# A fused transformer block on one core: five steps of 128, 128, 256, 256 and 256 tokens in place of four steps of 256

## What is computed

```python
xn = _rmsnorm(x, mix_norm_w[l]); proj = xn @ w_in[l]        # q, k, v, gates ...
o_da = diff attention, o_gla = gated linear attention, o_xa = attention over mem
merged = g0 * (o_da @ w_br_da) + g1 * (o_gla @ w_br_gla) + g2 * (o_xa @ w_br_xa)
x = x + merged @ w_out[l]
q = xb @ w_q; s = q . sub_keys; top_s, top_i = top_k(s, 16)   # per head, two halves
best_s, best_j = top_k(cand_s, 16); idx = ...; g = softmax(best_s)
u = expert_u[idx]; v = expert_v[idx]
act = gelu(einsum('thkd,td->thk', u, xb))
x = x + einsum('thk,thkd->td', g * act, v)
```

## Time and profile before

| | |
|---|---|
| median of 3 runs | 3866.09 us (3856.25 to 3876.32) |
| the profiled execution | 3867.53 us |
| its span, first to last instruction | 3865.7 us |
| mean granted TensorE clock | 0.862 |
| busy, share of span | PE 75%, PEld 38%, DVE 59%, ACT 17%, POOL 30% |
| weight blocks loaded | 360 of 512.0 KB |
| read from memory and written | 1286.51 MB and 12.58 MB |

### The profile page before, as it was taken

The page is one execution under the profiler, slowest core; times in us unless marked ns, Lnnn a source line. Parts: engine busy times, 40 slices in busy tenths (PEclk is TensorE's granted clock), DMA queues, the critical chain, the costliest instruction groups (busy, mean ns, idle before and its releaser), DMA issues. The chain is left out here.

```text
span 3865.7 us, 31929 instructions
## 1 busy us (share of the span) xinstructions
PE 2892.5 (75%) x11208; PEld 1470.0 (38%) x11208; DVE 2281.4 (59%) x5605; ACT 674.8 (17%) x1244; POOL 1146.2 (30%) x1044
## 2 busy tenths in 40 slices
PE   6779886789988857779987765787897854555555
PEld 3458652335645312335644322333563521111111
DVE  1230187775445786775454777676555598665665
ACT  1220111531111111531111111441111000000000
POOL 0000003343332233433332233343332324443442
PEclk9779997889998978989998887898999966777777
DMA  4114449999999898899999898889999969999998
GB/s 154 68 60 153 169 134 383 359 410 384 398 410 374 353 353 347 346 377 376 399 391 355 333 350 352 333 344 350 384 418 368 398 266 379 421 421 389 420 421 367
DMA packets 212159, 1301.22 MB, mean 337 GB/s; under 512 B 25360, under 2 KB 26144, under 8 KB 80928
## 3 DMA queue, kind: packets, MB, share of 16 engines
q0 software_dynamic: 149760, 1082.20, 69.7%
q1 hardware_dynamic: 62240, 216.99, 15.1%
HBM read 1286.51 MB, written 12.58 MB: 336 GB/s over the span
## 5 line engine op out<-in xcount | busy, mean ns | idle before, releaser
L582 POOL DMA_INDIRECT rowbuf<-in_peer_uv,idx x848 | 943.2, 1112 | 2266.6 <-PE acc L844 1542.9
L844 PE MATMUL acc<-rowbuf,diag 128*64 128x512 f32 x3392 | 1010.6, 707 | 474.3 <-DVE diag L1474 471.3
L1464 DVE CUSTOM_DVE_ANT_0 rowbuf<-rowbuf,xr 128x1024 f32<-128x1024 f32 x848 | 1021.3, 1223 | 529.1 <-DMA rowbuf<-in_peer_uv,idx 525.3
L844 PEld LDWEIGHTS acc<-rowbuf,diag 128*64 128x64 f32 x3392 | 246.1, 154 | 1053.9 <-DVE diag L1474 581.1
L1086 ACT ACTIVATE acts<-dots 128x2 f32<-128x2 f32 x512 | 104.1, 203 | 2476.3 <-DVE dots L1464 2416.8
L640 PE MATMUL bank<-xnT,W 128*128 128x256 f32 x1792 | 413.4, 387 | 0.0
L1474 DVE TENSOR_SCALAR diag<-consts,acts,gw 128x64 f32<-128x64 f32 x1024 | 285.6, 351 | 182.1 <-ACT acts L1086 109.1
L626 PE MATMUL bank<-W,xnT 128*128 128x512 f32 x832 | 384.7, 612 | 3.1 <-DVE xnT L1174 2.6
L640 PEld LDWEIGHTS bank<-xnT,W 128*128 128x128 f32 x1792 | 340.1, 193 | 98.7 <-issue 54.2
L844 PE MATMUL acc<-kv,diag 128*64 128x512 f32 x560 | 210.9, 780 | 115.7 <-DVE diag L1474 108.5
L640 PE MATMUL bank<-arena,W 128*128 128x256 f32 x1024 | 242.3, 394 | 45.9 <-DMA W<-in_w_blocks 43.4
(11 more groups left out here) (165 smaller groups left out, 2297.2 us busy)
## 6 DMA issues: line engine op xcount, KB each, us to landing
W<-in_w_blocks SPq DMA_DIRECT2D x360, 512.0 KB
rowbuf<-in_peer_uv,idx POOLq DMA_INDIRECT x848
xs<-in_x SPq DMA_DIRECT2D x16, 512.0 KB, 9.6
xr<-x SPq DMA_DIRECT2D x32, 256.0 KB, 7.9
out_y<-xs SPq DMA_DIRECT2D x8, 512.0 KB, 7.4
x<-arena SPq DMA_DIRECT2D x8, 512.0 KB
fin<-out_y POOLq DMA_DIRECT2D x8, 512.0 KB
out_y<-fin POOLq DMA_DIRECT2D x8, 512.0 KB, 10.2
```

Of the source, the lines that this page charges most:

```text
L582: pool.indirect_dma_start(rows[SLOT[g]], None, a["peer_uv"], bass.IndirectOffsetOnAxis(ap=idx[:, at // NB, at % NB:at % NB + 1], axis=0)). ...
L844: mm = pe.matmul(acc[HP * j:HP * (j + 1), h * HALF:(h + 1) * HALF], diag[:, c % DIAGS, j, :], v[:, D + h * HALF:D + (h + 1) * HALF], start ...
L1464: dve.tensor_tensor_reduce(out=u, in0=u, in1=xr[:, t, j, :], scale=1.0, scalar=0.0, op0=ALU.mult, op1=ALU.add, accum_out=dots[:, c % QS, j ...
```

## The change

The step sizes become a list, `TILES = (1, 1, 2, 2, 2)` tiles, and everything that was counted as `NT * (n - 1)` or `T` is counted by `tiles(n)`, `tile0(n)` and `ntok(n)`. The same eight tiles are mixed, ranked and gathered in the same order, with the same number of gathers, pairs and rankings. What differs:

- the first 256 tokens are two steps of 128. A step of one tile has half the attention units, chunks, streams of `token_major`, and streams 128 columns instead of 256 in `channel_major`; there are as many weight blocks in it as in a step of 256;
- the rows of tile 0 are used while tile 1 is mixed, those of tile 1 while tiles 2 and 3 are mixed; from there on a step of 256 is mixed beside the 256 gathers of the step before, as it was;
- `spread()` halves the lengths of the places in `BY_TOKENS` for a step of one tile, and starts at `GQK` of the next step behind a step that has no second ranking;
- the ring has one row buffer more for tile 0, and for tiles 2 to 7 as many as it had for them;
- ScalarE waits at `WQ` 0 for the stores of both tiles of `x2`, where it waited for one at `WQ` 0 and one at `WQ` 1.

```diff
+TILES = (1, 1, 2, 2, 2)
+STEPS = len(TILES)
...
+def tiles(n):
+
+    return TILES[n - 1] if n else NT
...
+def tile0(n):
+
+    return sum(TILES[:n - 1])
...
+    if n < STEPS:
+        kv, kt, q, rest = front(n + 1)
+        out += kv + ranks[0][:2] + kt + ranks[0][2:] + q
+        return out + (ranks[1][:2] + rest + ranks[1][2:] if tiles(n) > 1 else rest)
+    return out + sum(ranks, [])
...
 def row_buffers(g):
+    n = step_of(g)
     if n == STEPS:
         return [*range(ROWS, ROWS + EXTRA), *range(ROWS)]
-    return list(range(ROWS)) + kv[n + 1 if rel < KV_UNTIL else n + 2:]
+    share = (g - 2 * pair0(n)) / (tiles(n) * NB)
+    kv = [ROWS + i for i in range(KV_ROWS) if kv_step(i) > n + 2 or kv_step(i) == n + 2 and share < KV_UNTIL]
+    return list(range(ROWS)) + kv
...
+BY_TOKENS = ("GQK", "XQ", "GV", "GR", "GATE", "BR", "WO", "WQ", "SC", "K", "V", "Q", "OT", "GO", "SU")
...
+    def span(p):
+        return SPAN[p[0]] * (tiles(p[1]) / NT if p[0] in BY_TOKENS else 1)
+
+    def start(m):
+        if tiles(m) > 1:
+            return places.index(("R", m, 1, 0))
+        return places.index(("GQK", m + 1)) if m < STEPS else len(places)
...
+        count = tiles(m + 1) * PAIRS if m + 1 < STEPS else LAST_RANK
...
             def token_major(job, out_of):
-                    for t in range(NT):
+                    for t in range(tiles(job[1])):
...
             def channel_major(job, rhs):
+                nk = ntok(job[1])
...
-                        mm = pe.matmul(ps[:, c * T:(c + 1) * T], w[:, k, :], rhs[:, k, :], start=k == 0, stop=k == KC - 1)
+                        mm = pe.matmul(ps[:, c * nk:(c + 1) * nk], w[:, k, :], rhs[:, k, 0:nk], start=k == 0, stop=k == KC - 1)
...
                 for j in range(4):
                     if j == 2 and n < STEPS:
                         square_x(n + 1)
-                    if j < 2:
-                        act.wait_ge(x2_out[j], 16 * n)
-                    copy(("WQ", n, j), qp[:, j % 2, :], 1024)
+                    if j == 0:
+                        for g in range(tile0(n), tile0(n + 1)):
+                            act.wait_ge(x2_out[g % NT], 16 * (g // NT + 1))
+                    copy(("WQ", n, j), qp[:, j % 2, 0:4 * ntok(n)], 4 * ntok(n))
...
                 begin(n)
-                rank(n, 1)
+                if tiles(n) > 1:
+                    rank(n, 1)
```

More of the change, by code:

```diff
@@ L237, in kv_released @@
 def kv_released(n):
-    g = [g for g in range(GATHERS) if SLOT[g] == ROWS + n - 1 and step_of(g) < STEPS]
+    mine = [ROWS + i for i in range(KV_ROWS) if kv_step(i) == n]
+    g = [g for g in range(GATHERS) if SLOT[g] in mine and step_of(g) < STEPS]
     return g[-1] // 2 + 1 if g else 0
@@ L259, in spread @@
     for m, (at, end) in enumerate(zip(starts, starts[1:] + [len(places)])):
-        total = sum(SPAN[p[0]] for p in places[at:end])
-        count = NT * PAIRS if m + 1 < STEPS else LAST_RANK
+        total = sum(span(p) for p in places[at:end])
+        first = pair0(m + 1)
+        count = tiles(m + 1) * PAIRS if m + 1 < STEPS else LAST_RANK
         so_far = 0
         for p in places[at:end]:
-            SINCE[p] = NT * PAIRS * m + count * so_far / total
-            so_far += SPAN[p[0]]
-            BEFORE[p] = NT * PAIRS * m + count * so_far / total
+            SINCE[p] = first + count * so_far / total
+            so_far += span(p)
+            BEFORE[p] = first + count * so_far / total
 spread()
@@ L591, in x1_back, with store @@
                 pool.dma_start(fin[:, :], y_tiles[g]).then_inc(fin_in, 16)
-            def store(n, t):
-                g = NT * (n - 1) + t
+            def store(g):
                 pool.wait_ge(y_ready, g + 1)
                 pool.dma_start(y_tiles[g], fin[:, :]).then_inc(y_out, 16)
[L598 to L611, removed]
+            for g in range(SEQ // P):
+                if g == tile0(STEPS):
+                    pool.wait_ge(*filled(("WQ", STEPS, 3)))
+                pool.wait_ge(route_done, g + 1)
+                for k in range(NB):
+                    if k == ROWS:
+                        if g:
+                            store(g - 1)
+                        x1_back(g)
+                    gather(NB * g + k)
+            store(SEQ // P - 1)
         @block.tensor
@@ L668, in project_front @@
                 channel_major(("GQK", n), xnT)
-                for t in range(NT):
+                for t in range(tiles(n)):
                     turn(("QT", n, t), [qn[:, t, 2 * h:2 * h + 2, :].rearrange("p a b -> p (a b)") for h in range(DA_H)],
@@ L1228, in memory_attention @@
+                dve.tensor_tensor(flat(gkd(n)), flat(gkd(n)), flat(gqk(n)[:, 2:4, :]), ALU.mult).then_inc(gla_ops, 1)
             def memory_attention(n):
-                for t in range(NT):
+                for t in range(tiles(n)):
                     job = ("XS", n, t)
@@ L1368, in route @@
                 picks.upto(("WO", n, 1))
-                after(norm_rows(2 * n + 1))
-                for t in range(NT):
+                after(norm_rows(2 * n + 1, tiles(n)))
+                for t in range(tiles(n)):
                     dve.scalar_tensor_tensor(xn2[:, t, :], xs[:, t, :], st2[:, 4 + t:5 + t], w_ffn[:, :], ALU.mult, ALU.mult).then_inc(xn2_ready, 1)
@@ L1379, in route @@
                     dve.wait_ge(*evacuated(("SC", n, j)))
-                    rows = [(t, i) for t in range(NT) for i in range(4)]
+                    rows = [(t, i) for t in range(tiles(n)) for i in range(4)]
                     top16([sc[:, t, i, :] for t, i in rows], [tv[:, t, 4 * j + i, :] for t, i in rows], [ti[:, t, 4 * j + i, :] for t, i in rows],
```

460 lines of the change are left out of this document (243 added, 217 removed).

## The result

| | before | after |
|---|---|---|
| median | 3861.17 us (3851.58 to 3876.32, 4 runs) | 3900.22 us (3892.24 to 3909.33, 4 runs) |
| the profiled execution | 3867.53 us | 3892.24 us |
| its span | 3865.7 us | 3890.5 us |
| weights' queue | 217.0 MB | 263.1 MB |

The changed kernel takes 1.0106 times as long, with a 95% interval of 1.0084 to 1.0129. It is slower, by some 40 us; 3930 had been forecast, in a range of 3855 to 3995. The profiled execution of after is the fastest of its four, so the two spans lie only 24.8 us apart.

The account below looks back on a forecast made before the run. Before 575.3 us the first step's mixing was taken to bind, after it transfers. The terms 348 + 500 + 620 + 2456 + 4 gave a span of 3928 us, forecast as 3930 us, 1.6% slower, range 3855 to 3995.

Parts of the forecast that it names:

- Part 1: First step with one tile, until the first gather can go: 348 us, bounds 320 to 370.
- The rival in which they don't: Short matmuls don't halve: 72 us more in Part 1, Part 2 still bound by transfers, 4002 us in all; chance 0.03.
- late weights: Rival, slower still: weights come late, Part 1 takes 380 and Part 2 545 us, span 4007 us; chance 0.13.
- Part 2: Tile 1 mixed beside the rows of tile 0: bound by transfers, 500 us, bounds 475 and 530.
- a bubble and the unevenness of the stages: In Part 2: the larger of both per stage gives 494 instead of 491 us; some 6 us at the start make 500.
- TensorE waiting for W in part 2: Profile sign: if TensorE waits for weights in Part 2, the prediction would be wrong; no size given.
- Part 3: Tiles 2 and 3 mixed beside the rows of tile 1: bound by the engines, 620 us, bounds 575 and 650.
- The rival in which part 3 goes at the pace of its transfers: Most pairs fall into idle engine time: Part 3 takes 546 us, the whole 3821 us; chance 0.12.
- 558 us where its sum breaks even: Limit for Part 3: under 558 us the rival of transfer pace decides, since the sum breaks even there.
- Part 4: The last three stretches: 2455.7 us as before, plus 4 us for the wait at `WQ` 0 for both x2 stores.
- The rivals that were faster or level: Part 3 at 546 us gives 3821 us (chance 0.12); costs ending low, Part 3 at 590, gives 3868 us (0.14).
- The sum, 3928 us: Span of the whole kernel: 348 + 500 + 620 + 2456 + 4 = 3928 us, 62 over 3865.7; forecast's chance 0.58.

## Why the prediction was right, point by point

- *Part 1, 348 us:* 354.0. The stages came out within 1 us of their terms but for K to Q, with the transposes (89.2 for 86.8), and the expert queries (42.8 for 37.9), where the working let the stage nearly halve; what held it up was not tried. One term is closer than its working: for `GQK` and memory attention, 69.3 us less half of 52.4 and less 10.8 is 32.3, not the 38.7 that stands in the sum, and 39.1 were measured. Short matmuls halve: 578 records in 66.0 us, 0.114 each, as the row of 16 said. The rule that was weighed against the row (the Trainium skill, "TensorE: Matmul & The Clock Gate", "Back-to-back issue gap") would have put 72 us more into this part, and the trace doesn't bear it out. The rival in which they don't falls, and so does that of late weights: in 0 to 354 us TensorE waited 1.6 us for W, in `channel_major`.
- *Part 2, 500 us:* 476.0. This is the largest miss of a single term. The transfers were sized well (0.97 x 476.0 = 462 us busy for 469), but the sum divided them by 0.955 and added a bubble and the unevenness of the stages on top. The bubble and the uneven stages, which the stage sum added, cost next to nothing with the share at 0.97. The prediction has the second set of weights cost its transfer time of 124 us in this part; without 15/16 of it the part is only 39.3 us shorter, 436.7 us, where "some 410" had been given to the engines. The prediction said that TensorE waiting for W in part 2 would speak against it. These are TensorE's waits for W from 354 to 830 us, in `channel_major` (L709), before a pair's `add` (L915), in the branches (L874) and in `token_major` (L694):

```profile
PE bank L709 <- DMA W<-in_w_blocks: 21.0, 5, 10.2
PE acc L915 <- DMA W<-in_w_blocks: 9.8, 7, 1.7
PE bank L874 <- DMA W<-in_w_blocks: 4.6, 3, 1.8
PE bank L694 <- DMA W<-in_w_blocks: 3.8, 3, 1.9
```

  It did wait, 39.2 us in all, with the DMA engines at 0.97. By its own words the prediction would be wrong here, though the account behind it holds; the sign was badly chosen. In a part that is bound by transfers, waits for W are one way in which the bound shows. With the pairs made short, these waits are longer (67.0 us in all) and the part is shorter; without the weights they are 5.5 us and it is shorter by 39.3. The 545 us of the rival of late weights would have needed a low share beside them.
- *Part 3, 620 us:* 622.6. The gates took 158.9 us, with 16 pairs, as said; the share was 0.79 for "near 0.75". The price of a pair, 2.15 us, is near the 1.9 and 2.0 that pairs moved into this part cost. The rival in which part 3 goes at the pace of its transfers (546) falls: 549.6 us are reached only with the pairs' work cut on both engines. The prediction names two limits for this part, 558 us where its sum breaks even and 575 under which "the change is a gain"; by its own sum 575 is no gain yet, and with 622.6 it makes no difference.
- *Part 4, 2455.7 + 4 us:* 872.7 + 889.1 + 676.1 = 2437.9. The 4 us for the wait at `WQ` 0 can be neither seen nor excluded: with the old step sizes the new code lies at 1.0009 (0.9995 to 1.0022), that is 2 us less to 8.5 more. The first stretch gave 14.0 us of it, 872.7 for 886.7, outside the 10 us that were allowed; the second gave 7.3, and the last took 3.5. `GQK` of step 4 begins 8.0 us after the ranking of tile 2 is done, where the same projection began 19.1 us after it before, which would mean that fewer pairs had piled up. But with 25 and 52 pairs left for part 3 it begins 16.8 and 16.9 us after, and the stretch is as short, 872.8 and 877.4 us. So this doesn't explain it. In the ten profiles with these step sizes the stretch is 872.7 to 879.3 us, and with the old step sizes in the new code 884.0: the gain comes with the step sizes, and its cause stays open.
- *The rivals that were faster or level:* they needed a part 3 of 546 and of 590 us, and it was never under 620 with its work whole.
- *The sum, 3928 us:* 3890.5. Part 2 gave 24 of the 37.5 us, part 4 22, part 1 took 6 and part 3 2.6. The sign rested on part 3 staying over 558 us and on part 2 being as long as its transfers, the second set of weights among them. Both held, but only 39 us of part 2 hang on that set. The 22 us of part 4 lie outside the argument.

The step that wasn't in the prediction is the one that pays. The start does come 221 us earlier, and parts 2 and 3 together take 264 us more than the stretch that they replace. About 50 of these come back when 40 of the 64 pairs are untied from the short step: with 24 pairs in part 2 and 104 in part 3 the same step sizes are ahead of the kernel before.

## What to carry to other kernels

Splitting the first step of a pipeline shortens its fill (here by 221 of 575 us), but pays a full set of weights in a part that may be bound by transfers, and leaves the next part bound by engines. Compare the DMA share of neighbouring parts: 0.97 beside 0.79 says that gathers are to be moved from one to the other, and that a step's fetch need not end where its neighbour's mixing ends. It doesn't say how many. The shares met with 25 pairs moved (0.90 and 0.89), and 40 were better; at 52 the gain was gone. What decides is what a pair gives back where it leaves against what it costs where it goes: 2.8 against 2.0 us from 25 to 40, 3.7 against 5.1 from 40 to 52, when the part it goes to had come to a share of 0.95. Where transfers bind, take their busy time with the best share the trace shows (0.97 to 0.98) and don't add stage by stage on top.

## What the runs showed of the hardware

- 16 DMA engines with two queues mixed held a share of 0.97 to 0.99 over 461 to 476 us, at 389 to 399 GB/s, while engines had waits of up to 19 us; before, the mixed stretches showed 0.91 to 0.95.
- A weight load of 192 ns is no floor for a matmul of 128 columns: in the gates of step 1, 576 loads are busy for 65.8 us in all, 0.114 each, because they overlap.
- The granted clock (here a mean over stretches at 2.4 and at 1.2 GHz) fell where TensorE had less to do: in part 3 from 0.91 to 0.85 when the pairs' columns were cut, in part 2 from 0.88 to 0.80 (there with VectorE's dots cut too). So the 80.7 and 82.5 us of matmul time that went are net. The pairs' own matmuls fell from 136.4 to 31.6 us in part 3 and from 141.6 to 37.7 in part 2, 105 and 104 less; the difference, 24 and 21 us, is what the other matmuls took more at the lower clock (those of L804, the same in number and shape, went from 341 to 440 ns in the mean in part 3).
- VectorE waited for the sigmoid of the gates before its diagonals for 68.4 us in part 3, in 6 waits, where the stretch of 834.7 us of before had 20.4 in 6. The gelus stand behind that sigmoid on ScalarE, and it waits for TensorE's gate projection. With 40 pairs moved the wait is 30.2 us. What it costs was not tried (L1559 is `weigh`, L1127 the sigmoid).

```profile
DVE diag L1559 <- ACT arena L1127: 68.4, 6, 14.1
```
